# Hybrid SSD and sparse attention layer on one core: attention gate tiles moved between the SSD groups, key compression blocks moved behind the last convolution, four convolution accumulators

## What is computed

```python
h = _rmsnorm(x, g_pre) * (1.0 + scale[:, None, :]) + shift[:, None, :]
z_ssm, xbc, dt_raw, q, kv, nsa_gate, z_att, merge_gate = jnp.split(h @ w_in, IN_SPLITS, axis=-1)
y_ssm = _mamba2_branch(z_ssm, xbc, dt_raw, ...) @ w_ssm_out      # 32 heads in 4 groups
y_nsa = _nsa_branch(q, kv, nsa_gate, z_att, ...) @ w_nsa_out
...
xbc = jax.nn.silu(_causal_dwconv(xbc, conv_w, conv_b))           # x, b, c columns
y = y.reshape(bsz, s, D_INNER) * jax.nn.silu(z)                  # then one norm per group
...
blk = kv[:, idx] + pos[None, None, :, None, :]                   # 15 blocks of 32 tokens per KV group
return jax.nn.silu(blk @ w1) @ w2
...
return o.reshape(bsz, s, ATT_WIDTH) * jax.nn.silu(z_att)
```

## Time and profile before

| | |
|---|---|
| times of three runs | 482.01, 480.33, 480.41 us |
| median | 480.41 us |
| the profiled execution | 482.09 us |
| its span, first to last instruction | 480.3 us |
| busy in the span | PE 449.0 us (93%), DVE 352.9 (73%), ACT 266.3 (55%), POOL 231.1 (48%) |
| mean granted clock of TensorE | 0.974 of full speed |

### The profile page before, as it was taken

The page is one execution under the profiler, slowest core; times in us unless marked ns, Lnnn a source line. Parts: engine busy times, 40 slices in busy tenths (PEclk is TensorE's granted clock), DMA queues, the critical chain, the costliest instruction groups (busy, mean ns, idle before and its releaser), DMA issues.

```text
span 480.3 us, 9912 instructions
## 1 busy us (share of the span) xinstructions
PE 449.0 (93%) x3656; PEld 412.0 (86%) x3656; DVE 352.9 (73%) x617; ACT 266.3 (55%) x520; POOL 231.1 (48%) x237
## 2 busy tenths in 40 slices
PE   2589999999999996999899999999999999999995
PEld 2287999999999986987799999988999999999874
DVE  0476789999999999958676676578787666549633
ACT  2235884655566555654678735566474464535441
POOL 0155653368688548672375632245344362344340
PEclk9789999999999998999989988999999999999999
DMA  8998543654524523417529630725756433356102
GB/s 288 421 413 324 181 133 127 209 187 132 174 69 135 184 102 98 167 45 280 199 74 383 215 124 0 263 96 185 249 174 226 129 129 125 108 185 244 48 0 87
DMA packets 22103, 82.99 MB, mean 173 GB/s; under 512 B 2460, under 2 KB 2850, under 8 KB 20898
## 3 DMA queue, kind: packets, MB, share of 16 engines
q1 hardware_dynamic: 22056, 82.37, 48.4%
HBM read 81.31 MB, written 1.05 MB: 171 GB/s over the span
## 4 chain that ended last, share of the span: by engine, by line
PE 69%; DVE 9%; issue 9%; POOL 5%; ACT 4%; DMA 3%; SPq 1%; DVEq 0%; ACTq 0%; POOLq 0%
PE gemm L694 15%; PE gemm L696 15%; PE gemm L695 15%; DMA w_ada_shift_scale<-in_w_ada 3%; PE y_or_o L900 2%; DVE w_lo L1193 2%; DVE conv_acc L1240 2%; ACT w_hi L929 2%; POOL w_lo L1535 2%; POOL seg_moving L1547 1%; PE score L864 1%; PE small L575 1%; PE y_or_o L782 1%; PE score L866 1%; PE gemm L653 1%
## 5 line engine op out<-in xcount | busy, mean ns | idle before, releaser
L1535 POOL TENSOR_TENSOR w_lo<-w_raw,w_hi 128x256 fp32r<-128x256 f32 (+1 forms) x117 | 131.9, 1133 | 181.5 <-ACT w_hi L929 147.7
L694 PE MATMUL gemm<-h_hi,w_hi 128*128 128x256 f32 x600 | 174.4, 291 | 1.5 <-DVE conv_acc L1240 1.0
L695 PE MATMUL gemm<-h_lo,w_hi 128*128 128x256 f32 x600 | 169.8, 283 | 0.0
L696 PE MATMUL gemm<-h_hi,w_lo 128*128 128x256 f32 x600 | 169.7, 283 | 0.0
L1193 DVE TENSOR_TENSOR w_lo<-w_raw,w_hi 128x768 fp32r<-128x768 f32 (+1 forms) x117 | 131.3, 1123 | 44.9 <-ACT w_hi L929 44.0
L929 ACT CAST w_hi<-w_raw 128x1024 fp32r<-128x1024 f32 x117 | 122.0, 1045 | 49.6 <-PE gemm L696 27.4
L694 PEld LDWEIGHTS gemm<-h_hi,w_hi 128*128 128x128 f32 x600 | 115.1, 192 | 3.9 <-issue 2.4
L695 PEld LDWEIGHTS gemm<-h_lo,w_hi 128*128 128x128 f32 x600 | 114.8, 191 | 0.6
L696 PEld LDWEIGHTS gemm<-h_hi,w_lo 128*128 128x128 f32 x600 | 114.6, 191 | 0.0
L694 PE MATMUL gemm<-ynorm_hi,w_hi 128*128 128x256 f32 x128 | 36.6, 286 | 0.0
L696 PE MATMUL gemm<-ynorm_hi,w_lo 128*128 128x256 f32 x128 | 35.8, 280 | 0.0
(11 more groups left out here) (259 smaller groups left out, 906.8 us busy)
## 6 DMA issues: line engine op xcount, KB each, us to landing
w_raw<-in_wpack SPq DMA_DIRECT2D x133, 512.0 KB, 4.3
w_ada_shift_scale<-in_w_ada SPq DMA_DIRECT2D x8, 1024.0 KB, 15.8
x_T<-in_xT SPq DMA_DIRECT2D x2, 512.0 KB, 6.0
x_residual<-in_x_tok SPq DMA_DIRECT2D x1, 1024.0 KB, 4.8
out_tok_dram<-out_tok SPq DMA_DIRECT2D x4, 256.0 KB, 2.1
consts<-in_consts SPq DMA_DIRECT2D x1, 272.0 KB, 22.0
cmp_bias_and_valid<-in_cmp_bias SPq DMA_DIRECT2D x1, 272.0 KB, 2.8
w_compress<-in_w_compress SPq DMA_DIRECT2D x1, 192.0 KB, 6.0
```

What stands on the lines that cost most here:

```text
L694: nc.tensor.matmul(bank[:, 0:SEQ], w_hi, hi[:, k0 + k, :], start=first, stop=False)
L695: nc.tensor.matmul(bank[:, 0:SEQ], w_hi, lo[:, k0 + k, :], start=False, stop=False)
L696: last = nc.tensor.matmul(bank[:, 0:SEQ], w_lo, hi[:, k0 + k, :], start=False, stop=end)
L1535: nc.gpsimd.tensor_tensor(WL[:, n % LO_SLOTS, c:1024], RAW[:, u % RAW_SLOTS, c:1024], WH[:, n % HI_SLOTS, c:1024], ALU.subtract).then_inc( ...
```

## The change

Each group gets a ninth unit, the attention gate tile `za` g, behind its `z` tiles; of the `za` tiles only 4 and 5 are left in front of `w1k`, so all units from 49 on keep their numbers. The steps of a group follow with b = 20 + 9g: `seg` of the second quad goes one unit behind `y` of the first, and its `ea` and `y`, and `ysq`, one unit later each. The steps `ysum`, `ssq` and the norm keep their distance from b. The four `blk0` steps move from units 18, 26, 34 and 42 to 45, 46, 47 and 48, behind the last `x` unit (43). `blk1` follows the groups (19, 28, 37, 46), `clear` goes from 47 to 49. The convolution gets four accumulators instead of two; two of them lie where half of `hid_v_T` lies, so `clear` waits for the last convolution gate before it zeroes that tile.

```diff
     for g in range(SSM_GROUPS):
-        units += [("x", TPG * g + j, 0) for j in range(TPG)] + [("z", TPG * g + j, 0) for j in range(TPG)]
-    units += [("za", j, 0) for j in range(6)]
+        units += [("x", TPG * g + j, 0) for j in range(TPG)] + [("z", TPG * g + j, 0) for j in range(TPG)] + [("za", g, 0)]
+    units += [("za", j, 0) for j in range(4, 6)]
...
-        b = 20 + 8 * g
+        b = 20 + 9 * g
         put(b, ("xt", (g, 0)))
         put(b + 1, ("xt", (g, 1)), ("seg", 2 * g))
         put(b + 2, ("ea", 2 * g))
-        put(b + 4, ("y", 2 * g), ("seg", 2 * g + 1))
-        put(b + 5, ("ea", 2 * g + 1))
-        put(b + 7, ("y", 2 * g + 1))
-        put(b + 8, ("ysq", g))
+        put(b + 4, ("y", 2 * g))
+        put(b + 5, ("seg", 2 * g + 1))
+        put(b + 6, ("ea", 2 * g + 1))
+        put(b + 8, ("y", 2 * g + 1))
+        put(b + 9, ("ysq", g))
         put(b + 10, ("ysum", g))
         put(b + ssq_after, ("ssq", g))
...
-        put(18 + 8 * g, ("blk0", g))
-        put(19 + 8 * g, ("blk1", g))
-    put(47, ("clear", 0))
+        put(45 + g, ("blk0", g))
+        put(19 + 9 * g, ("blk1", g))
+    put(49, ("clear", 0))
...
+ACCS = 4
...
-    ACC = place("conv_acc", [P, 2, SEQ], f32, at=over_at + 42 * kb)
+    ACC = place("conv_acc", [P, ACCS, SEQ], f32, at=over_at + 40 * kb)
...
-                    if ci >= 2:
-                        act.wait_ge(gated, max(v for k, v in TH_IDX.items() if k[0] in CONV and conv_index(*k) == ci - 2) + 1)
+                    if ci >= ACCS:
+                        act.wait_ge(gated, max(v for k, v in TH_IDX.items() if k[0] in CONV and conv_index(*k) == ci - ACCS) + 1)
...
                 elif what == "clear":
+                    pool.wait_ge(gated, TH_IDX[("x", 4 * TPG - 1)] + 1)
                     nc.gpsimd.memset(HVR[:], 0.0).then_inc(zeros, 1)
                     pool.wait_ge(blk_done[0], 16)
```

More of the change, by code:

```diff
@@ L959, in read_out @@
                     ci, col = conv_index(kind, j), conv_src(kind, j)
-                    if ci >= 2:
-                        act.wait_ge(gated, max(v for k, v in TH_IDX.items() if k[0] in CONV and conv_index(*k) == ci - 2) + 1)
-                    nc.scalar.activation(ACC[:, ci % 2, :], bank, ACT.Identity, bias=CW[:, 96 + col:97 + col],
+                    if ci >= ACCS:
+                        act.wait_ge(gated, max(v for k, v in TH_IDX.items() if k[0] in CONV and conv_index(*k) == ci - ACCS) + 1)
+                    nc.scalar.activation(ACC[:, ci % ACCS, :], bank, ACT.Identity, bias=CW[:, 96 + col:97 + col],
                                          scale=CW[:, 4 * col + 3:4 * col + 4]).then_inc(conv_acc, 1)
@@ L970, in read_out @@
                         act.wait_ge(gated, k - 1)
-                    nc.scalar.activation(TH[:, k % 2, :], ACC[:, ci % 2, :], ACT.Tanh).then_inc(th_full, 1)
+                    nc.scalar.activation(TH[:, k % 2, :], ACC[:, ci % ACCS, :], ACT.Tanh).then_inc(th_full, 1)
                 if kind in CONV:
@@ L1239, in read_out @@
                         s = 3 - tap
-                        ins = nc.vector.scalar_tensor_tensor(ACC[:, ci % 2, s:SEQ], bank[:, 0:SEQ - s],
-                                                             CW[:, 4 * col + tap:4 * col + tap + 1], ACC[:, ci % 2, s:SEQ],
+                        ins = nc.vector.scalar_tensor_tensor(ACC[:, ci % ACCS, s:SEQ], bank[:, 0:SEQ - s],
+                                                             CW[:, 4 * col + tap:4 * col + tap + 1], ACC[:, ci % ACCS, s:SEQ],
                                                              ALU.mult, ALU.add)
@@ L1252, in read_out @@
                         wait_y_out(dve, ("y", 2 * (prev[1] // TPG - 2) + 1))
-                    gate(prev, conv_dst(*prev), ACC[:, ci % 2, :])
+                    gate(prev, conv_dst(*prev), ACC[:, ci % ACCS, :])
                 if kind in CONV:
```

## The result

The changed kernel takes 485.32 us (median of 9 runs, 482.93 to 486.53), the kernel before beside it 481.21 us (median of 9). The ratio is 1.0079, with a 95% interval from 1.0063 to 1.0096. I had forecast 476.8 us and faster; it came out slower, and above the upper end of my range. The profiled execution has a span of 484.1 us, against 480.3 before: 3.8 us more. Ratios are of fast runs: single executions of e1, e2 and e9 that took 558, 1120 and 2467 us are left out of them.

What follows compares the result with a forecast made beforehand. VectorE's backlog was taken to set the pace, with PE waits and half clock worth 12.1 us. New losses of 5.2 + 1.7 + 1.6 = 8.5 us left 3.6 us won: 476.8 us, range 470.0 to 482.5.

Steps and rivals of the forecast that it cites:

- `x_dt` of group 1 to `x_dt` of group 3: VectorE's work over groups 1 and 2: 69.9 us, against 64.6 us that PE needs; some 1.2 us of waiting came on top.
- from there to the end of the blocks: VectorE, from the x_dt that starts group 3 to the last blk0 addition: 6.7 us, including two blk0 packets.
- half clock: TensorE granted half speed after the wait at w1k, as a 4.1 us wait brought before: 1.7 us added.
- `ssq` 3: Tail among the native units: PE waits for the read-out, squares and sums of the last group, taken as 1.6 us.
- slower: Outcome class for the whole kernel: a time over 482.8 us, given a chance of 0.14.
- waits some 1.2 us for the first convolution tiles of group 1, then works through: VectorE from group 1 on: after a 1.2 us wait, no further idle time until the blk0 additions end at 80.8.
- VectorE busy over 97% in groups 1 and 2: Sign expected in the profile after the change: VectorE almost without idle time in both groups.
- the packet of 2.0 us: Length of each blk0 packet on VectorE before w1k, taken from 4.0 us for eight additions.
- part 2: Blocks behind the last convolution: VectorE's blk0 additions end late, so PE waits 5.2 us in front of w1k.
- rival B: Block packets meet GpSimd, 0.8 to 1.3 us longer each; w1k waits 8 to 10 us; 479.6 to 482; 0.18 with no effect.
- part 1: Ninth unit and steps: groups take 32.3 us on PE; square root moving from decay gives back up to 3.1 us.
- C: Slower rival: VectorE 3 us later at w1k, late for y 7 and ssq; 16.6 us lost against 12.1, 484.8 us; chance 0.12.

Runs made afterwards that it cites:

- e1: Changed kernel with the four key compression blocks back among the groups (steps 18, 27, 36, 45): 480.94 us, ratio 0.9984 to the kernel before.
- e2: Kernel before with only the four blocks moved, behind units 45 to 48: 482.75 us, ratio 1.0022 to the kernel before.
- e9: Changed kernel with the norm steps written behind everything else of their unit: 480.11 us, ratio 0.9976 to the kernel before.
- e8: Changed kernel with the blocks in group 0 (steps 18, 21, 24, 27) and norm steps one unit later: 473.11 us, ratio 0.9829 to the kernel before.
- e7: Changed kernel with all four block packets in group 0 (steps 18, 21, 24, 27): 476.89 us, ratio 0.9915 to the kernel before.
- e11: Changed kernel with GpSimd's quad 6 cb_decay and cb_decay_across and quad 7 seg_moving cut to 8 of 128 columns, output incomplete: 482.24 us, one run.
- e5: Changed kernel with the norm steps (yn, ynhi, ynlo) one unit later: 479.45 us, ratio 0.9958 to the kernel before.
- e6: Changed kernel with the third block packet beside the fourth (steps 45, 46, 48, 48): 484.64 us, ratio 1.0058 to the kernel before.
- e4: Changed kernel with two accumulators instead of four: 485.36 us, ratio 1.0077 to the kernel before.
- e3: Kernel before with four accumulators instead of two, clear waiting for the last convolution gate: 482.6 us, ratio 1.0017 to the kernel before.
- e12: Kernel before, eight units in a group, with only its blocks moved behind units 18, 21, 24 and 27: 481.37 us, ratio 1.0006.
- e10: Changed kernel with blocks in group 0, norm steps one unit later and ssq 3 two units later: 479.94 us, ratio 0.9959 to the kernel before.

## Why the prediction was wrong

The table holds the clock that I had set up (VectorE against PE from the start of group 1, here 128.47) beside what the windows above show, in us.

| Term | predicted | measured |
|---|---|---|
| first `x_dt` behind group 1's transposes | 3.0 | 2.6 |
| `x_dt` of group 1 to `x_dt` of group 3 | 1.2 + 69.9 = 71.1 | 75.1 |
| from there to the end of the blocks | 6.7 | 8.2 |
| VectorE at `w1k` | 80.8 | 85.8 |
| PE behind PE's own work of 75.6 | 5.2 | 10.4 |
| half clock | 1.7 | 2.7 |
| `ssq` 3 | 1.6 | 1.8 |

10.4 is 214.46 - 128.47 - 75.6. 2.7 is the half clock's price as read above from e8, and 1.8 the gap of 2.0 less 0.12. The last three rows make 14.9 us, 6.4 more than the 8.5 that I had; 476.7 + 6.4 is 483.1, and the span is 484.1, so 1.0 us is in none of these terms. `w1k` started at 214.46 where I had said about 209. My range ended at 482.5, and I had given "slower" 0.14.

**The step that failed first** is "waits some 1.2 us for the first convolution tiles of group 1, then works through". VectorE's busy time between the two `x_dt` is 26.85 + 43.44 = 70.3 us; my 69.9 held 1.4 us of pauses from the kernel before (66.0 busy of 67.4), so the work is 1.8 us more than I had. Most of that is one split: between the two `x_dt` the changed list holds 17 of them and the list before 16, for the 13 of 896 columns in the earlier trace rows count one that began at 128.29, ahead of the window. I had called the numbers equal; one more is 1.3 us. The rest of the 4.0 us is idle time: 4.8 us, of which I had allowed 1.2 and the 1.4. All but 1.1 us of it lies in group 1. I had added up two groups, 69.9 against 64.6, as if the work could be spread over them at will. It can't: in group 1 VectorE has less work than PE gives it time for, and what it doesn't do there is not made up. "VectorE busy over 97% in groups 1 and 2" was one of my signs: it held in group 2 (97.5%) and not in group 1, 28.28 of 33.10 us, 85%. The blocks were moved out of groups 0 to 2 into exactly the stretch that has none to spare. e7 shows it the other way: the same additions, put into group 0, halve the idle time of groups 0 and 1, and the kernel is 8 us faster, with the half clock and the collision of the next paragraph gone too.

**The second is the packet of 2.0 us** in part 2. Its source was an average of additions in the kernel before, some beside GpSimd and some not. The third packet meets three GpSimd instructions and takes 3.92 us; e11 puts the collision at 2.7 of these. The fourth packet, alone, takes 1.26, so both take 5.2 where I had 4.0: 1.2 of the 1.5 us in the third row. I had a row that pointed there (2.27 at 188.38) and rival B for it, and left the sum as it was because that row was only 0.3 over my value. The Trainium skill, page "SBUF — State Buffer", section "Who interferes with whom", has a VectorE instruction with two inputs in SBUF and a GpSimd instruction that reads SBUF block one another, the later one for all of the other's length. The trace agrees: three additions of 0.34 us are shown with 1.1 to 1.33 us, beside GpSimd instructions of 1.42, 1.33 and 2.11 (two). I should have counted GpSimd instructions beside each packet instead of widening an average.

**The third is in part 1**, where I wrote that the square root moves "away from `decay`" and followed no further what moves with it. The wait for `y` 5 did fall, by 2.5 us (4.1 to 1.6). But I read only the table loads' new neighbours, and not where the reciprocal, `y_tmp` and `ynorm_hi` now stand: ahead of `cb_decay` on VectorE and of `decay_across` on ScalarE. This is most of the 1.1, 0.9 and 1.9 us in front of `y` 3, `ea` 4 and `y` 5, of which my list of signs had excluded the last. e5 and e9, which change only this, gain 5 to 6 us. That is more than these waits, 3.9 us: 2.7 us of e5's gain are the place of the half clock. And it is not VectorE's idle time that they shorten. From group 0's start to `w1k` that is 10.6 us in the changed kernel, 10.2 in e5 and 11.0 in e9, while its busy time falls from 107.4 to 105.0 and 104.7 us, with the same instructions but for one `ynorm_lo` in e5. Why the same list took less time to run is open.

**The half clock** came at `w1k`, as I said, but for 6.8 us and for a price of 2.7. I took the length of the earlier trace rows for the only one, and both are seen in this stage among the versions of the changed kernel: 3.4 in e6, e9 and e11, 6.8 in e4 and e5, none in e1, e7 and e8. I have no rule for which.

**What held**: `y` 4 starts without a wait; the MLP's transposes don't wait; the wait in front of `w1k` is ended by `cmp_blocks` and the one in front of `ssq` 3 by GpSimd's `y_sq`, 1.8 us against 1.6; `clear` costs nothing; four accumulators are worth nothing (e4). Of the rivals, C came nearest with its 484.8 us, and by luck in part: it priced the new losses at 16.6 us, and they are 14.9 by the table. VectorE was late by 5 us rather than 3, while `y` 7 and `ssq` 3, which C charged with 5 us together, cost 1.8.

## What to carry to other kernels

When work is moved on an engine that is nearly full, count its slack stretch by stretch: idle time in one group can't be spent in the next, and the right place for free work is the window where the engine is seen idle (here group 0), even if it is long before its consumer. When the spacing of groups changes, list for every step that keeps its old offset what it now stands ahead of on each engine; a short copy that waits for another engine, in front of an exponential that doesn't, cost more here (5 to 6 us, e5 and e9) than moving the square root gave back (2.5 us at `y` 5). For small VectorE additions, count GpSimd's instructions beside them instead of taking an average.

## What the runs showed of the hardware

The additions of 64x120 elements take 0.33 to 0.37 us with GpSimd silent (the fourth packet of the changed kernel, the one at 115.24 of e7). They grow with the GpSimd instruction that they meet: 0.35 to 0.55 us beside GpSimd's own additions (the kernel before, at 94.61), 0.7 to 0.8 beside its `w_lo` of 0.8 to 0.9 us (before, at 188.38), 1.0 to 1.4 beside `cb_decay`, `cb_decay_across` and `seg_moving` of 1.1 to 1.4 us (the changed kernel, e2). Beside GpSimd's memset of `hid_v_T`, which reads nothing, they stay at 0.35 (e6), and with the three instructions cut to 8 columns at 0.34 (e11).

Half clock is not tied to a fixed amount of waiting. e1, e7 and e8 wait at some of the same places as the changed kernel and have none there. Near 285 us, in a part of the program that no experiment touches, a stretch of 6.8 us stands in the profiled executions of before, the changed kernel, e3 and e6, one of 3.4 us in those of e7 to e12, and none in those of e1, e2, e4 and e5. From the second pair of MLP transposes to the end of the span it is 240.2 us in the changed kernel and 239.0 in e1, e4 and e5, so the 6.8 us cost about 1.2 there, and the 6.8 us at `w1k` 2.7; neither is half the length. One profiled span may thus differ by that much from another for no reason of the edit, and I have read losses from the gaps and the ratios, and not from the spans alone.

A matmul step can be held by a bank that it only needs empty. The `small` steps take turns on two banks; three times (`ea` 6 and `ssq` 2 in the changed kernel, the transposes in e10) PE waited 2.3 to 4.4 us for a reader of a bank whose data had been there long before.
